# Two MLP units issued inside the output projection, around the turn of its last tile

## What is computed

```
x   = x + mix @ w_out                       # output projection, K = 1024
h2  = rmsnorm(x, ln2)
x   = x + square(relu(h2 @ mlp_up)) @ mlp_down     # D_FF = 4096
y   = rmsnorm(x, ln_f)
```

## Time and profile before

| | |
|---|---|
| median of three runs | 1996.0 us (1994.66 to 1996.02) |
| the profiled execution | 1996.08 us, its span 1994.1 us |
| TensorE busy | 1835.0 us, 92% of the span |
| VectorE, ScalarE, GpSimd busy | 42%, 27%, 13% |
| share of the last chain that is TensorE | 38% (the largest) |
| last unit of the projection ends, about | 1210.3 us into the span |
| first matmul of the MLP stage | 1219.61 us |
| granted clock over the whole span | 0.944 of full speed |

### The profile page before, as it was taken

How to read it: one execution, slowest core, us unless ns; L and a number is a source line. 1 busy time by engine, 2 the same in 40 slices (tenths; PEclk the granted TensorE clock), 3 DMA queues, 4 the chain that set the end, 5 groups by cost and what they waited for, 6 DMA issues and landing times. The chain is left out here.

```text
span 1994.1 us, 27838 instructions
## 1 busy us (share of the span) xinstructions
PE 1835.0 (92%) x11634; PEld 1545.9 (78%) x11634; DVE 837.6 (42%) x1501; ACT 542.7 (27%) x1028; POOL 268.0 (13%) x323
## 2 busy tenths in 40 slices
PE   3999989978888778999999998999999999999998
PEld 2988889967778665555554787888888888888886
DVE  4543261134444334454443453444444444444447
ACT  4122231132321235444444322211111111212212
POOL 7200000034442010001100000101010101011100
PEclk9989999969888658999999998999999999999999
DMA  4010013030000200000000301111111111111102
GB/s 124 24 33 24 24 55 135 18 90 2 2 28 3 64 26 1 0 1 21 22 0 1 132 0 64 43 43 43 43 43 43 43 43 43 43 43 43 44 34 108
DMA packets 31503, 79.50 MB, mean 40 GB/s; under 512 B 11390, under 2 KB 17870, under 8 KB 26098
## 3 DMA queue, kind: packets, MB, share of 16 engines
q1 hardware_dynamic: 31314, 77.63, 11.5%
q0 software_dynamic: 64, 0.09, 0.0%
HBM read 69.62 MB, written 10.12 MB: 40 GB/s over the span
## 5 line engine op out<-in xcount | busy, mean ns | idle before, releaser
L252 PE MATMUL ps<-mix_hi,wbuf 128*128 128x364 f32 (+1 forms) x768 | 253.3, 330 | 3.4 <-PEq L3021 3.4
L254 PE MATMUL ps<-mix_hi,wbuf 128*128 128x364 f32 (+1 forms) x768 | 253.0, 329 | 0.0
L253 PE MATMUL ps<-mix_lo,wbuf 128*128 128x364 f32 (+1 forms) x768 | 252.9, 329 | 0.0
L2951 DVE TENSOR_TENSOR x<-x,ps 128x512 f32<-128x512 f32 x272 | 180.5, 686 | 113.2 <-PE ps L254 112.0
L252 PE MATMUL ps<-wbuf,mlp_hid_hi 128*128 128x512 f32 x512 | 201.2, 393 | 0.0
L254 PE MATMUL ps<-wbuf,mlp_hid_lo 128*128 128x512 f32 x512 | 199.4, 390 | 0.0
L253 PE MATMUL ps<-wbuf,mlp_hid_hi 128*128 128x512 f32 x512 | 199.2, 389 | 0.0
L2936 DVE TENSOR_TENSOR mlp_hid_lo<-mlp_rect,mlp_hid_hi 128x364 fp32r<-128x364 f32 (+1 forms) x96 | 72.1, 751 | 285.8 <-ACT mlp_hid_hi L2857 285.8
L2908 POOL TENSOR_TENSOR mlp_rect<-mlp_rect 128x364 f32<-128x364 f32 (+1 forms) x96 | 76.3, 794 | 763.5 <-ACT mlp_rect L2880 763.5
L252 PEld LDWEIGHTS ps<-mix_hi,wbuf 128*128 128x128 f32 x768 | 145.7, 190 | 4.1 <-issue 3.6
L253 PEld LDWEIGHTS ps<-mix_lo,wbuf 128*128 128x128 f32 x768 | 145.3, 189 | 0.5
(11 more groups left out here) (561 smaller groups left out, 3569.2 us busy)
## 6 DMA issues: line engine op xcount, KB each, us to landing
out_raw<-in_w_up SPq DMA_DIRECT2D x16, 1024.0 KB, 4.8
mlp_raw_down<-in_w_down SPq DMA_DIRECT2D x16, 1024.0 KB, 4.8
feat_raw<-in_w_feat SPq DMA_DIRECT2D x12, 512.0 KB, 4.5
spare<-in_w_token SPq DMA_DIRECT2D x4, 1056.0 KB, 5.3
ln_x<-in_x_prompt SPq DMA_DIRECT2D x8, 512.0 KB, 8.3
ck<-in_cache_nsa SPq DMA_DIRECT2D x16, 256.0 KB, 2.9
out_raw<-in_w_out SPq DMA_DIRECT2D x4, 1024.0 KB, 4.8
x<-in_x_prompt SPq DMA_DIRECT2D x8, 512.0 KB, 6.1
```

The lines of the kernel that those rows point to most:

```text
L252: pe.matmul(out, lhs[0], rhs[0], start=first, stop=False)
L253: pe.matmul(out, lhs[0], rhs[1], start=False, stop=False)
L254: return pe.matmul(out, lhs[1], rhs[0], start=False, stop=last)
L2951: dve.tensor_tensor(part, part, m.ps[:, u % 8, :], ALU.add).then_inc(added, 1)
```

## The change

Two units of the MLP, up 0 (0, 0) and (0, 1), are taken from the head of `mlp_products` and issued by TensorE in `output_and_norm`: the first ahead of `turn(TS)`, the second behind it. Their results lie in banks 0 and 1 until the other stage reads them. The projection's banks are shifted by two so that units 16 and 17 lie in banks 2 and 3, and counts of `product` in the MLP stage are two less (`after`).

```diff
--- before.py
+++ after.py
@@ -2580,6 +2580,10 @@
         squared, var_ready, std_ready, vec = sem("squared"), sem("var"), sem("std"), sem("vec")
         normed, turned, evacuated, hi_made, lo_made = sem("normed"), sem("turned"), sem("evacuated"), sem("hi_made"), sem("lo_made")
         up_hi, up_lo = sem("up_hi"), sem("up_lo")
+        up = [m.wbuf[:, x * KT * FG:(x + 1) * KT * FG].rearrange("p (k n) -> p k n", k=KT) for x in range(2)]
+
+        def bank(i):
+            return m.ps[:, (i + EARLY) % 4, :]
 
         def chunk(t, c):
             return t[:, :, QUARTER * (c - 2):QUARTER * (c - 1)]
@@ -2672,7 +2676,7 @@
                         dve.wait_ge(x_loaded[t], 16)
                     dve.wait_ge(product, i + 1)
                     part = m.x2[:n, t, HALF * h:HALF * (h + 1)]
-                    dve.tensor_tensor(part, part, m.ps[:n, i % 4, :], ALU.add).then_inc(evac, 1)
+                    dve.tensor_tensor(part, part, bank(i)[:n, :], ALU.add).then_inc(evac, 1)
 
                 def normalise(t):
                     n = ROWS[t]
@@ -2742,12 +2746,27 @@
                         pe.wait_ge(evac, i - 3)
                     for k in range(KT):
                         lo = mix_lo[:, k, t * P:(t + 1) * P] if t < TS else last_lo[:, k, :]
-                        last = triple(pe, m.ps[:, i % 4, :], [mix_hi[:, k, t * P:(t + 1) * P], lo], [x[:, k, :] for x in weights[h]],
+                        last = triple(pe, bank(i), [mix_hi[:, k, t * P:(t + 1) * P], lo], [x[:, k, :] for x in weights[h]],
                                       k == 0, k == KT - 1)
                     last.then_inc(product, 1)
                     if i in turned_after:
                         turn(turned_after[i])
+
+                def early_up(u):
+                    o, w = GROUPS_N[u]
+                    pe.wait_ge(up_lo, 1)
+                    pe.wait_ge(lo_made, -(-(o + w) // P))
+                    pe.wait_ge(evac, len(units) - 3 + u)
+                    for k in range(KT):
+                        triple(pe, m.ps[:, u, :w], [x[:, k, 0:P] for x in up],
+                               [x[:, k, o:o + w] for x in (mix_hi, mix_lo)], k == 0, k == KT - 1)
+
+                early_up(0)
                 turn(TS)
+                early_up(1)
+
+
+EARLY = 2
 
 
 def mlp_products(nc, m):
@@ -2810,9 +2829,13 @@
 
             i = turn_of[kind, g]
             if i >= 2:
-                eng.wait_ge(product, ends[phases[i - 2]])
+                eng.wait_ge(product, after(ends[phases[i - 2]] - 1))
 
         begin = {"up": (0, 0), "down": (TS, 0)}
+
+        def after(u):
+            return u + 1 - EARLY
+
         final = [TS] + list(range(TS))
 
         def prompt_part(b):
@@ -2831,7 +2854,7 @@
                     if made(kind, g) > 1:
                         sp.wait_ge(lo_made[kind], made(kind, g) - 1)
                     if kind == "down" and g:
-                        sp.wait_ge(product, units.index(("down", g - 1, TS, 0)) + 1)
+                        sp.wait_ge(product, after(units.index(("down", g - 1, TS, 0))))
                     src = m.a["w_" + kind][g].rearrange("p a n -> p (a n)")
                     sp.dma_start(raw[kind][:], src).then_inc(loaded[kind], 16)
                 sp.dma_start(gain[:], m.a["ln_f"]).then_inc(gain_loaded, 16)
@@ -2873,8 +2896,9 @@
                         if g:
                             round_weights("down", g - 1)
                         if g >= 2:
-                            act.wait_ge(product, ends["down", g - 2])
-                    act.wait_ge(product, u + 1)
+                            act.wait_ge(product, after(ends["down", g - 2] - 1))
+                    if u >= EARLY:
+                        act.wait_ge(product, after(u))
                     if rank[u] > RT:
                         act.wait_ge(hid_lo, rank[u] - RT)
                     act.activation(rect[:, (rank[u] - 1) % RT, :w], m.ps[:, u % 8, :w], ACT.Relu).then_inc(rectified, 1)
@@ -2942,7 +2966,7 @@
                         rest_of_weights("up", g + 2)
                     if (a, b) == (3, 0) and g == NG - 2:
                         rest_of_weights("down", g + 1)
-                    dve.wait_ge(product, u + 1)
+                    dve.wait_ge(product, after(u))
                     if g:
                         dve.wait_ge(added, rank[u] - DOWNS)
                     elif a == TS:
@@ -2962,7 +2986,7 @@
 
             @block.tensor
             def _(pe):
-                for u, (kind, g, a, b) in enumerate(units):
+                for u, (kind, g, a, b) in list(enumerate(units))[EARLY:]:
                     x = g % 2
                     if (a, b) == begin[kind]:
                         if made(kind, g):
```

## The result

The changed kernel takes 1985.64 us (median of 14 runs, 1981.38 to 1990.81), the kernel before 1996.01 us in the same runs. The ratio is 0.9953, with a 95% interval of 0.9936 to 0.9969: between 6.2 and 12.8 us faster, 9.4 in the middle. The profiled execution took 1987.41 us, with a span of 1985.5 us in place of 1994.1.

What follows compares the result with a forecast made beforehand. TensorE, busy 92% of the span, was taken as the bound. 10.66 us removed behind the barrier, less 1.75 at the barrier and 0.1 at unit 2's start, gains 8.8: 1996.08 to 1987.3 us, range 1985.6 to 1991.0.

Steps and rivals of the forecast that it cites:

- VectorE's tail: Tile 8 taken out on VectorE behind its turn, claimed done at 1218.38 us as before.
- The cover ahead of the turn: TensorE's 4.77 us hole before tile 8's turn: unit 0's 4.00 us fit at no cost, 0.7 us left.
- The barrier now being TensorE's: At the stage barrier: it waits for TensorE instead of VectorE and opens 1.75 us later.
- The clock: TensorE around turn and barrier: granted clock taken as 1.00 throughout, since its longest idle falls to 1.2 us.
- the slow part of unit 0: First MLP unit behind the barrier, run at lowered clock: 2.66 us of the 8.8 us gain, which no longer exists.
- one row for it, 939: Trace place at 939 to 941 us: busy 0.77 of 2.00 us, clock stays 1.00; supports no fall.
- one against it, 1018: Trace place at 1018.00 to 1020.40 us: busy 1.15 of 2.40 us, clock then 0.50; supports a fall.
- The clock falling at one of the new short gaps: Rival, gaps at turn or barrier: 1990.8 or about 1990.0 us, 13% for one; 1993.5 us, 3% for both.
- Weights too late: Rival at unit 6: up 1's weights arrive late, about 2002 us with the landing at 26 us; 2%.
- That the change does nothing: Rival in the MLP: something else holds its pace, the 8.8 us return as TensorE waits, 1996 us; 2%.
- the main case: Whole kernel: the forecast of 1987.3 us, own range 1985.8 to 1988.8, given 78%.
- the play of 1.4 us: Whole program's time: one of three runs was 1.4 us lower, taken as the time's own play.

Runs made afterwards that it cites:

- e1: Against the kernel before, only unit 0 is moved, ahead of the turn; unit 1 stays behind the barrier: 1991.98 us, ratio 0.9981.
- E5: The change with a third unit, unit 2, also moved, behind unit 1: 1984.44 us, ratio 0.9945 to the kernel before.
- e9: Against the kernel before, unit 0 moved ahead of the turn and 12 matmuls with unused results (filler) added behind it: 1990.94 us, ratio 0.9969.
- e3: The change with both units issued ahead of the turn: 1987.33 us, ratio 0.9959 to the kernel before.
- e6: The kernel before with 24 matmuls whose results nobody uses (filler) added ahead of the turn: 1997.37 us, ratio 1.0008.
- e10: The kernel before plus 36 matmuls with unused results (fillers), 24 ahead of the turn, 12 behind it: 1994.22 us, ratio 0.9983.
- e7: The change with up 1's weights rounded behind unit 5's relu instead of unit 2's, their low half also later: 1992.56 us, ratio 0.9992 to the kernel before.
- e8: The change with the first of unit 1's eight slices moved ahead of the turn: 1985.39 us, ratio 0.9947 to the kernel before.
- e2: Against the kernel before, only unit 0 is moved, and behind the turn: 1992.05 us, ratio 0.9984.
- e4: The change with both units issued behind the turn: 1992.77 us, ratio 0.9980 to the kernel before.

## Why the prediction was right, step by step

Measured from tile 7's turn, since that is where the two profiles can be laid on each other:

| step | predicted | measured |
|---|---|---|
| unit 0 starts | 6.33 | 6.32 |
| turn of tile 8 starts | 11.26 | 11.26 |
| idle ahead of it | 0.7 | 0.78 |
| unit 1 starts | 12.05 | 11.90 |
| idle at the barrier | 1.2 | 1.21 |
| unit 2 starts | 17.6 | 17.37 |
| low half of up 1 ready before unit 6 | 6.3 | 6.2 |
| unit 6 starts (D) | 33.6 | 33.36 |

The weights' row is from VectorE's timeline of the change; its end is 1231.31, and unit 6 starts at 1237.51:

```profile
1229.02 2.29 DVE L2938 TENSOR_TENSOR wbuf<-out_raw,wbuf 128x2048 fp32r<-128x2048 f32 x1 [1.53 <-ACT wbuf L2872]
```

The predicted 8.8 us are 9.0 in D. Of the 0.2 more, 0.15 is the turn, which I had priced at 0.79 us by tile 7's; behind tile 8's at full clock unit 1 began 0.64 us after its start. One thing was overlooked: VectorE's tail was to end "as before", and it ended 0.41 us sooner, since the turn that feeds it ran at full clock. It cost nothing here, because TensorE holds the barrier; in e1 it is 0.41 us of the gain.

**The cover ahead of the turn** was right. E1 moves one unit there, and the turn's place does not change by more than 0.01 us.

**The barrier now being TensorE's** was right, and was priced right. E5 shows the consequence, a third unit worth nothing, and e9 the price of what unit 1 brings: the work of unit 1 is 4.0 us and D falls by 2.02 (35.38 to 33.36), because the rest is what TensorE ends later than VectorE.

**The clock** was right for this kernel, with an account that holds only for the change as a whole. The prediction reads "It fell after the 4.77 us without work" and books 2.66 us as the slow part of unit 0. It leaves open that the 3.41 us hole would have done the same alone, and for e1 and e3 I then expected that it would not; for e6 I left it open. E1, e3, and e6 have it closed at the front and open at the back, and the clock fell in all three. In the change both are closed. That the clock would stay up over the short gaps rested on one row for it, 939, and one against it, 1018; it was a bet, priced as one. The fillers give the clock its own price: 42.36 to 39.38, 2.98 us, of which 2.60 are the two units behind the barrier and 0.38 the turn, which at full clock is shorter by 0.40 (0.71 against 1.11), and VectorE's tail and the barrier with it.

So the 9.0 us, added in the order e10, e9, the change, are 2.98 for the clock, 4.00 for unit 0, and 2.02 for unit 1. The 2.98 is the price in these two profiles: e3's unit behind a fall lost 1.28 us and not 2.66. In another order the parts would differ: unit 1 on top of e1 is worth 4.74, since it closes the second hole as well.

**The rivals.** The clock falling at one of the new short gaps did not happen; at 0.78 and 1.2 us it stayed at 1.00 in the profiles of the change, e5, e7, e9 and e10, and at 0.27 and 1.21 us in e8's. The Trainium skill ("TensorE: Matmul & The Clock Gate", A second HAM failure mode: psum-queue depth-cycling) tells of short idles that do it; the trace does not agree at this place. Weights too late did not happen, and e7 shows that the prediction's way of pricing it was sound, but for one thing: a wait of 5 us also costs the clock, 1.58 us here. By that, its time of 2002 would have been longer by about as much, an estimate. That the change does nothing is out.

**The total.** 1987.3 was forecast and 1985.64 measured. The medians differ by 10.4 us, the ratio says 9.4, and D says 9.0; the interval of 6.2 to 12.8 holds them all, and the forecast gain of 8.8 too. The gain was worked out rightly; that the time itself fell inside the range was luck. It lies 0.04 us above the range's lower end of 1985.6, and below the 1985.8 to 1988.8 given for the main case. The step that was wrong is the play of 1.4 us, taken from three runs: the 14 runs of the change lie 9.4 us apart, those of the kernel before 15.7 us (1990.49 to 2006.21). By that play it is chance as well that the profiled run, 1987.41, is within 0.1 us of the forecast.

## What to carry to other kernels

Idle time of the bounding engine can have two prices, its length and what it costs in clock afterwards. Here the second was only saved when both long holes of the place were closed; close them all, if need be with matmuls for nobody, before judging what one of them is worth. Work moved ahead of a barrier is free only up to the moment at which another engine would have released it; past that, it trades one for one, which tells how much to move. To measure 1 us in a program whose time plays by 10, take a distance between two marks in the trace that encloses the whole effect of the change and as little else as possible.

## What the runs showed of the hardware

The same hole of 3.41 us had different prices. TensorE's first unit behind it took 6.80 us in e1 and 6.79 in e6, and 5.32 us in e3, where the clock was back about 3 us sooner; at full clock it takes about 4.0. Behind e7's longer wait of 5.08 us it took 5.58. So a clock price read from one profile was good to a factor of two here, and it did not follow the length of the hole. What decides it is not shown.

The play of the whole program goes with the clock. The fastest of the change's 14 runs, 1981.38 us, was granted 0.951 on average, the slowest, 1990.81 us, 0.944, and over the 14 the correlation of time with granted clock is -0.97. Code ahead of the change, equal in all of these kernels, put the start of tile 7's turn at different times: 1199.43 in e2, 1204.15 in the change, 1210.34 in e9.

A barrier with the semaphore clear behind it cost TensorE 1.21 to 1.23 us when TensorE was last or nearly so (the change, e2, e4, e5, e7 to e10).
